# The first layer's norms over two sequences: four output tiles, the norm and the next stage's first tiles in the order of the sequences

## What is computed

```python
for i in range(2):
    h_lat = modulate(rms_norm(x, norm1_g[i]), sh1, sc1)
    h_ctx = modulate(rms_norm(ctx, norm1_g[i]), sh1c, sc1c)
    y_ctx, y_lat = mixer(h_ctx, h_lat, ...)          # ends with  [...] @ w_out
    x = x + g1 * y_lat
    x = x + g2 * conv_ffn(modulate(rms_norm(x, norm2_g[i]), sh2, sc2), w_up, ..., w_down)
    if i == 0:
        ctx = ctx + g1c * y_ctx
        ctx = ctx + g2c * conv_ffn(modulate(rms_norm(ctx, norm2_g[i]), sh2c, sc2c), w_up, ..., w_down)
```

## Time and profile before

| | us |
|---|---|
| median of 3 runs | 2531.45 (2529.63 to 2534.05) |
| the profiled execution | 2535.02 |
| its span on the core | 2533.3 |
| PE busy in the span | 2447.2 (97%) |
| site A, from tile 4 of ev_out to the end of up0's tile 3 | 53.5 |
| site B, from tile 4 of down0's rest to the end of od_in's tile 3 | 43.2 |

### The profile page before, as it was taken

One profiled execution on the slowest core, in us unless ns is written; L12 is line 12 of the kernel. 1 busy time (PEld: TensorE's weight loads), 2 busy tenths in 40 slices (PEclk: granted clock), 3 DMA queues, 4 the chain that ended last, 5 costly groups with the idle time before them and its releaser, 6 DMA issues.

```text
span 2533.3 us, 47380 instructions
## 1 busy us (share of the span) xinstructions
PE 2447.2 (97%) x17994; PEld 2239.4 (88%) x17994; DVE 1767.3 (70%) x2863; ACT 1177.7 (46%) x1816; POOL 107.4 (4%) x161
## 2 busy tenths in 40 slices
PE   8999999999999999989999999999999999989998
PEld 6867777778798999987999998999989999978997
DVE  4878699988747866685665867665557657676665
ACT  4554422223545444454544544544545446465443
POOL 2221000000000000003000000000000000000000
PEclk9999999999999999998999999999999999999999
DMA  7423255554424555322555532555425554322553
GB/s 298 142 100 134 92 195 181 186 182 154 168 92 142 191 183 164 120 93 68 166 182 186 166 114 68 174 180 189 148 66 175 188 177 150 101 85 76 199 179 120
DMA packets 119643, 378.18 MB, mean 149 GB/s; under 512 B 11591, under 2 KB 28999, under 8 KB 119120
## 3 DMA queue, kind: packets, MB, share of 16 engines
q1 hardware_dynamic: 105936, 327.58, 38.9%
q0 software_dynamic: 12528, 47.62, 5.5%
q10 hardware_dynamic: 1040, 1.05, 0.1%
HBM read 375.15 MB, written 1.05 MB: 148 GB/s over the span
## 4 chain that ended last, share of the span: by engine, by line
PE 84%; DVE 9%; ACT 4%; issue 2%; DMA 0%; DVEq 0%; ACTq 0%; SPq 0%
PE gb L597 22%; PE gb L598 21%; PE gb L599 21%; DVE w_lo L566 3%; PE mb L676 2%; PE mb L2653 1%; PE gb L1162 1%; ACT w_hi L560 1%; PE gb L2634 1%; PE mb L599 1%; PE mb L597 1%; PE mb L598 1%; DVE W L2386 1%; PE gb L648 1%; PE gb L650 1%
## 5 line engine op out<-in xcount | busy, mean ns | idle before, releaser
L597 PE MATMUL gb<-Xs,w_hi 128*128 128x256 f32 (+1 forms) x3584 | 1098.1, 306 | 18.2 <-DVE w_lo L566 5.2
L599 PE MATMUL gb<-Xs,w_lo 128*128 128x256 f32 (+1 forms) x3584 | 1084.4, 303 | 0.0
L598 PE MATMUL gb<-Xs,w_hi 128*128 128x256 f32 (+1 forms) x3504 | 1054.5, 301 | 0.0
L560 ACT ACTIVATE w_hi<-raw 128x1024 fp32r<-128x1024 f32 x616 | 646.8, 1057 | 778.0 <-PE gb L599 728.1
L566 DVE TENSOR_TENSOR w_lo<-raw,w_hi 128x1024 fp32r<-128x1024 f32 x616 | 746.7, 1223 | 221.5 <-ACT w_hi L560 214.6
L597 PEld LDWEIGHTS gb<-Xs,w_hi 128*128 128x128 f32 x3584 | 679.5, 190 | 73.5 <-issue 28.9
L599 PEld LDWEIGHTS gb<-Xs,w_lo 128*128 128x128 f32 x3584 | 679.4, 190 | 31.3
L598 PEld LDWEIGHTS gb<-Xs,w_hi 128*128 128x128 f32 x3504 | 664.6, 190 | 26.6 <-issue 1.4
L598 PE MATMUL gb<-Fs,w_hi 128*128 128x256 f32 (+1 forms) x1016 | 294.4, 290 | 0.0
L599 PE MATMUL gb<-Fs,w_lo 128*128 128x256 f32 (+1 forms) x936 | 262.4, 280 | 0.0
L597 PE MATMUL gb<-Fs,w_hi 128*128 128x256 f32 (+1 forms) x936 | 262.3, 280 | 0.0
(11 more groups left out here) (404 smaller groups left out, 2851.6 us busy)
## 6 DMA issues: line engine op xcount, KB each, us to landing
raw<-in_up SPq DMA_DIRECT2D x264, 512.0 KB, 3.2
raw<-in_down SPq DMA_DIRECT2D x96, 512.0 KB, 3.7
R<-in_mod_later POOLq DMA_DIRECT2D x80, 512.0 KB, 3.9
raw<-in_gdn_in SPq DMA_DIRECT2D x64, 512.0 KB, 3.2
raw<-in_down SPq DMA_DIRECT2D x48, 384.0 KB, 3.9
raw<-in_hgrn_in SPq DMA_DIRECT2D x32, 512.0 KB, 4.1
raw<-in_ev_in SPq DMA_DIRECT2D x24, 512.0 KB, 4.4
raw<-in_gla_in SPq DMA_DIRECT2D x24, 512.0 KB, 4.1
```

The source lines that it names most:

```text
L560: nc.scalar.activation(w_hi[:, slot], raw[:, slot], ACT.Identity).then_inc(*hi_ready.inc())
L597: nc.tensor.matmul(to, w_hi[:, w_slot, k, :], x_hi, start=start, stop=False)
L598: nc.tensor.matmul(to, w_hi[:, w_slot, k, :], x_lo, start=False, stop=False)
L599: return nc.tensor.matmul(to, w_lo[:, w_slot, k, :], x_hi, start=False, stop=stop)
```

## The change

At both sites the work after output tile 3 is done for one sequence after the other.

- PE makes output tiles 4 to 7 for sequence 0 only (`half_out`), then for sequence 1 (`gemm_out`); the warming matmuls are gone. Four blocks k into tile 4's second half come the two matmuls of ones for sequence 0.
- The next stage's tiles 0 to 2 are made for sequence 0 in all 8 blocks k, with the ones for sequence 1 after block 2 (A) or 4 (B), and then for sequence 1. At B tile 3's half of sequence 0 stands between.
- DVE and ACT norm sequence 0 (`dve_seq_norm`, `act_seq_norm`), and between its steps they split the next weight tiles 0 to 2, read tiles 4 to 7 of sequence 1 and square them; then they norm sequence 1. ACT now writes the rounded part itself, and for odd m DVE applies scale and shift once more (`low`).
- At B the wide part's sum of tiles 4 to 7 is closed and added to `X` on its own (8 more operations on DVE), since the two halves of the rest go to other banks (`rest_bank`).

```diff
+        def pe_seq_stats(pe, s):
+            pe.wait_ge(*sums_kept.due("pe"))
+            nc.tensor.matmul(sbank[:, SEQ[s]], ones[:, :], sq_sum(2 * T)[:, SEQ[s]], start=True, stop=False)
+            pe.wait_ge(*sq_ready.due("pe", 4 if s else 8))
+            nc.tensor.matmul(sbank[:, SEQ[s]], ones[:, :], squares_at(KC - 1, 2 * T)[:, SEQ[s]], start=False, stop=True).then_inc(*sum_done.inc())
...
+            if by_seq:
+                for u in range(AHEAD):
+                    pe.wait_ge(*lo_ready.due("pe"))
+                    pe.wait_ge(*gemm_taken.free("pe"))
+                pe_seq_group(pe, range(AHEAD), 0, stats_at=2)
+                pe_seq_group(pe, range(AHEAD), 1, last=range(AHEAD))
...
+            for m in BY_SEQ:
+                pe.wait_ge(*half_taken.due("pe"))
+                for k in range(KC):
+                    last = pe_block(gb[:, m % BANKS, SEQ[1]], m % SLOTS, k, Xs[:, k, SEQ[1]], Xs[:, KC + k, SEQ[1]], k == 0, k == KC - 1)
+                    if m == BY_SEQ[0] and k == 3:
+                        pe_seq_stats(pe, 0)
+                last.then_inc(*gemm_out.inc())
...
+        def act_seq_norm(act, layer, norm):
...
+            for j, m in enumerate(BY_SEQ):
+                if j < 3:
+                    act_tile(act)
+                shifted(2 * j, 0)
+                if m == BY_SEQ[3]:
+                    square(m, 1)
+                shifted(2 * j + 1, 0)
+                if m < BY_SEQ[3]:
+                    square(m, 1)
+            root(1)
+            act_tile(act)
+            for m in range(KC):
+                shifted(m, 1)
...
+        def dve_seq_norm(dve, part, layer, norm, mods_done, beside=None, banks=None):
...
+            for j, m in enumerate(BY_SEQ):
+                if j < 3:
+                    dve_tile(dve)
+                for k in (2 * j, 2 * j + 1):
+                    if k + 2 < KC:
+                        scaled(k + 2, 0)
+                    low(k, 0)
+                    if j == 3 and k % 2 == 0:
+                        sums(KC - 2, 1)
+                        taken(m)
+                if j < 3:
+                    taken(m)
+                    if j < 2:
+                        sums(m, 1)
...
+            pe_seq_group(pe, range(AHEAD), 0, stats_at=4, last=range(2))
+            pe.wait_ge(*lo_ready.due("pe"))
+            pe.wait_ge(*gemm_taken.free("pe"))
             for k in range(KC):
-                pe.wait_ge(*h_ready.due("pe"))
-                for u in range(AHEAD):
-                    n = T if u < 2 else 2 * T
-                    last = pe_block(gb[:, u, 0:n], u, k, Xs[:, k, 0:n], Xs[:, KC + k, 0:n], k == 0, k == KC - 1)
-                    if k == KC - 1:
-                        last.then_inc(*gemm_out.inc())
-            tile(3, 2 * T)
+                pe_block(gb[:, 3, SEQ[0]], 3, k, Xs[:, k, SEQ[0]], Xs[:, KC + k, SEQ[0]], k == 0, k == KC - 1)
+            pe_seq_group(pe, (2, 3), 1, last=(2, 3))
```

More of the change, by code:

```diff
@@ L624, in tile @@
                 last.then_inc(*gemm_out.inc())
-            peel = SLOTS if ready or tiles == SLOTS else 0
+            peel = SLOTS if ready or by_seq or tiles == SLOTS else 0
             if ready:
                 pe_group(pe, 0, n, ready)
-            for u in range(AHEAD if ready else 0, peel):
+            if by_seq:
[4 more added lines that the diff above has]
+                pe_seq_group(pe, range(AHEAD), 1, last=range(AHEAD))
+            for u in range(AHEAD if ready or by_seq else 0, peel):
                 tile(u)
@@ L785, in act_squares, with square, root, shifted @@
             sq_added.due("act")
+        def act_seq_norm(act, layer, norm):
+            use_table(LN_EXP)
+            for m in range(BY_SEQ[0]):
+                act_tile(act)
+                act.wait_ge(*gemm_taken.due("act"))
+                if m > 2:
+                    act.wait_ge(*sq_added.due("act"))
+                nc.scalar.activation(squares_at(m, 2 * T) if m else sq_sum(2 * T), X[:, m, :], ACT.Square, scale=1 / 32).then_inc(*sq_ready.inc())
+            def square(m, s):
+                if s:
+                    act.wait_ge(*gemm_taken.due("act"))
+                    if m > BY_SEQ[1]:
+                        act.wait_ge(*sq_added.due("act", 2 if m == BY_SEQ[2] else 1))
+                else:
+                    act.wait_ge(*half_taken.due("act"))
+                    act.wait_ge(*sq_added.due("act"))
+                nc.scalar.activation(squares_at(m, 2 * T)[:, SEQ[s]], X[:, m, SEQ[s]], ACT.Square, scale=1 / 32).then_inc(*sq_ready.inc())
+            def root(s):
+                act.wait_ge(*sum_done.due("act_sum"))
+                alink(act, nc.scalar.activation(W[:, 2, SEQ[s]], sbank[:, SEQ[s]], ACT.Ln, bias=eps[:, 0:1]))
+                nc.scalar.activation(W[:, 3, SEQ[s]], W[:, 2, SEQ[s]], ACT.Exp, scale=-0.5).then_inc(*rstd_ready.inc())
+            def shifted(m, s):
+                act.wait_ge(*normed.due("act"))
+                t = W[:, 4 + m % 4, SEQ[s]]
+                affine_of = dict(bias=modv[:, layer, 24 * norm + m, s:s + 1], scale=modA[:, layer, norm, m, s:s + 1])
+                last = nc.scalar.activation(Xs[:, m, SEQ[s]], t, ACT.Identity, **affine_of)
+                if m % 2 == 0:
+                    last = nc.scalar.activation(t, t, ACT.Identity, **affine_of)
+                last.then_inc(*affine.inc())
+            for m in BY_SEQ:
+                square(m, 0)
+            root(0)
+            act.wait_ge(*mod_ready.due("act"))
+            for j, m in enumerate(BY_SEQ):
[8 more added lines that the diff above has]
+            root(1)
+            act_tile(act)
+            for m in range(KC):
+                shifted(m, 1)
+            sq_added.due("act")
```

136 lines of the change are left out of this document (115 added, 21 removed).

## The result

The changed kernel is slower: 2556.67 us, the median of four runs (2552.89 to 2558.35), against 2530.59 for the kernel before (four runs). The ratio is 1.009, 95% interval 1.0076 to 1.0104, that is 19 to 26 us. On a second chip it was 1.0083 (1.007 to 1.0097; 2553.46 against 2532.11). The forecast was 2545.5 with a range up to 2552: the sign and the mechanism held, the size didn't.

The account below looks back on a forecast made before the run. PE was taken to bound the kernel, busy for 2447.2 of 2533.3 us. New waits at the sites (+9.4) and the clock (+4.8) made +14.2, taking the median from 2531.45 to 2545.5 us, range 2538 to 2552.

Parts of the forecast that it names:

- The rounds: Norm of sequence 0 at both sites: DVE and ACT take turns, 5.0 us a round, from 4.8 to 5.1.
- The waits at the groups: PE idle ahead of the next stage's first group, until DVE reads tile 6: 6.4 us at A, 8.9 at B.
- The last wait at B: PE waits 8.4 us ahead of od_in's tile 3 for its `w_lo`, which DVE makes behind the whole norm.
- The sum without the clock: Both sites up to the end of tile 3: A gains 0.3 us, B loses 9.7, together +9.4.
- splitting: Matmuls of 512 columns made as two of 256 at both sites: 0.002 us a pair, 0.6 us in all.
- The clock: Half-speed matmuls behind each of the three new waits: three times 1.6, 4.8 us, from 0 to 10.
- Behind the sites: After tile 3 of od_in: no term in the sum; only rival 4 claimed a loss there.
- rival 4: Behind the sites: ACT and DVE reach the rotations 9 us later, two clock stretches each; +20, 2552 us, chance 0.12.
- Rivals 1 to 3: Clock holds or returns: 2540.8, chance 0.12; round of 3.8 us: 2536.5, chance 0.07; faster as built for: 2517, chance 0.04.
- from a profile to a median: Whole kernel: profiled 2535.02 becomes 2549.2, so the median 2531.45 plus 14.1 becomes 2545.5 us.

Follow-up runs that it names:

- e6_lo3_early: Changed kernel with tile 3's `w_hi` ahead of sequence 1's root and its `w_lo` out from behind the norm, at B alone; 2547.07 us, ratio 1.0049.
- e4_warm_in_waits: Changed kernel with unread warm matmuls in PE's waits: 7 ahead of up0's first group, 9 ahead of od_in's, 8 ahead of its tile 3; 2544.35 us, ratio 1.005.
- e1_after_again: The changed kernel as it is, run again beside the kernel before; 2553.46 us, ratio 1.0083.
- e5_taken_first: Changed kernel with DVE taking the bank ahead of each round's `w_lo` and ACT squaring right behind its `w_hi`; 2544.60 us, ratio 1.0034.
- e7_both_orders: Changed kernel with both edits, those of e5_taken_first and e6_lo3_early; 2535.64 us, ratio 0.9999.
- e9_keeps_ahead: e7_both_orders plus warm matmuls (two ahead of up0's group, five ahead of od_in's), copies of tiles 0 and 1 and two `w_lo` ahead of the decays; 2532.99 us, ratio 1.0007.

## Why the prediction was right in kind and short in size

- **The rounds: right.** 5.0 us forecast, 4.84 to 4.96 measured. The `tensor_scalar` with two operands per partition took 0.40 us, not the 0.49 of the earlier trace rows; with 0.40 the forecast's own terms give 4.97. The bounds of 4.8 to 5.1 held.
- **The waits at the groups: right.** 6.4 and 8.9 us forecast, 6.40 and 8.54 measured, with the releaser named.
- **The last wait at B: right.** 8.4 forecast, 7.70 measured, released by `w_lo` of tile 3; e6_lo3_early takes it away by moving that one instruction.
- **The sum without the clock: right at the sites.** +9.4 forecast, +9.2 in e4_warm_in_waits. One reading in it was slightly off, without effect: matmuls of 256 columns stand 0.117 us apart (0.35 us for three in the earlier trace rows) and not 0.1177, so splitting costs 0.2 us or less and not 0.6.
- **The clock, the term that was mis-sized.** 4.8 us forecast as three times the 1.6 of the earlier trace rows. The rows behind the three waits lose 1.8, 1.6 and 2.4 in the first profile, and over both sites the three profiles lose 5.8, 5.8 and 7.1, mean 6.2. The shape of the earlier trace rows, one short stretch behind each wait, was carried over to waits of two to three times the length; the last one was followed by 5.2 us at half clock. The medians say more still: 9.1 us lie between e1_after_again and e4_warm_in_waits. Of these 6.2 are at the sites and 0.5 between the swap and the warm matmuls (1.65 - 1.15); the other 2.4 the profiles don't place, and the intervals of the two runs leave the 9.1 open by some 5 us either way.
- **Behind the sites: set to nothing, and wrong.** The sum ended at tile 3. In every profile the changed kernel loses 1.65 us more up to the warm matmuls ahead of up1, 1.15 of it without the clock's part, among it 0.59 for the third swap; the half-clock stretch near 803 us then makes the warm matmuls ahead of up1 take 4.21 instead of 3.60. This is rival 4 in part: it had the right place (the rotations come late) and 0.12 of the chance. Read as 9.4 + 9.6 for two clock stretches at each wait, its +20 leaves about 1 for what is lost behind the sites; measured were 6.2 for the clock and 1.65 + 0.4 behind, so the profiles lie between the forecast and this rival.
- **Rivals 1 to 3: out.** The clock fell behind each wait, the rounds were long, and no site gained.

Put together the terms become 9.2 + 6.2 + 1.65 + 0.4 = 17.5 us where the forecast had 14.2, and the spans of the three profiles of each kernel are on average 17.8 apart, so between profiles next to nothing is missing. **What stays open** is the step from there to the medians, 21.3 us on the second chip (interval 17.7 to 24.6) and 26.1 on the first. I took 14.1 us over from a profile to a median as if the two moved alike. They did not: the first profiled execution of before stood 4.4 us above the median of the result's four runs, that of the changed kernel 3.8 under its own, and 26.1 is 17.9 + 4.4 + 3.8. Added to the 2531.45 of before, 17.5 would have been 2549, inside the range; what put the measured 2556.67 above 2552 is this step more than the clock's 1.4 and the 2.05 behind the sites. The mean granted clock of all executions beside e1_after_again was 0.984 for before and 0.978 for the changed kernel; the rest is likely clock in places that come and go, but no run shows which. How much of it is the scatter of so few runs isn't shown either.

## What to carry to other kernels

When two engines work from lists in turns, lay the lists side by side and count the hand-overs in a round: the length of a round is the sum of both parts between the hand-overs, and putting each list's step for the other one first (e5_taken_first) took a good fifth off (3.8 and 3.9 us where it was 4.8 to 5.0) without removing any work. A step that splits one wide operation so that the matrix engine can go on earlier pays only if the other engines' lists are short enough behind it too. Here, with the waits of 6.4, 8.5 and 7.7 us down to 1.9, 4.3 and none (e7_both_orders), the kernel was level with the one before: PE gained 3.4 us up to the first swap and lost 3.0 behind it, where the rotations are. And warming that fills a hole is worth keeping in mind as part of what is removed: put back into the new waits it was worth 9 us of 21. Last, one profile isn't a median: take the difference of two profiles over to the medians only after seeing where each profiled execution lies among its runs.

## What the runs showed of the hardware

- Behind waits of PE of 6.4, 8.5 and 7.7 us the granted clock was 0.50 in three profiles out of three, for 3.9, 3.6 and 5.2 us of matmuls in the first and 5.6, 4.4 and 5.6 in the third; behind 2.0 us in e5_taken_first it was 1.00, as the window from 288.90 shows, and behind 4.3 us it was 0.50 for part of the next window:

```profile
288.90:292.30 3.40, 3.40 (x28) 3.39 (x29) 2.60 (x8) 1.95 (x5) 0.00 (x0) 1.00 0.48 154
669.00:672.40 3.40, 3.40 (x19) 3.40 (x20) 2.66 (x8) 1.95 (x5) 0.00 (x0) 0.59 0.52 154
```

- The same wait need not have the same effect. Behind the 2.97 us in ev_in the clock fell in all three profiles of before, and not in the first of the changed kernel, whose matmuls at 236.88 and 237.10 stand 0.22 us apart; in its third it fell for 6.8 us. Behind the 3.09 us in e9_keeps_ahead it was 0.50 for 6 us. The Trainium skill (TensorE: Matmul & The Clock Gate, "HAM oscillation") has a burst behind a long wait begin at the low clock; the three long waits agree with it, with 18, 17 and 24 matmuls at half speed in the first profile.
- A VectorE `tensor_scalar` of 128x256 with two operands per partition took 0.40 to 0.41 us, as long as a `tensor_tensor` of that shape (0.42).
